# Attention steps reordered, sample scores in every step, the last head from wide to narrow, output weights split earlier, projection tiles prepared two ahead

## The chip, the cores and the metric

The kernel runs on one core of one Trainium2 chip. The metric is the device time of one execution in microseconds (us). A step below is one of the 32 rounds of the attention loop; a tile is 128 rows of tokens. The engines are TensorE (PE, its weight loads PEld), VectorE (DVE), ScalarE (ACT), GpSimd (POOL), and SyncE (SP), which here only issues DMAs.

## What is computed

One layer on a prompt of 1024 tokens and on a sample group of 8 sequences with 8 new tokens each, all in float32. The model width is 1024.

```python
z = rmsnorm(x) @ w_in                       # q, k, v for 4 heads (2 x 64 wide), u and v_a of the gate
s1, s2 = q1 @ k1.T / 8 + rel, q2 @ k2.T / 8 + rel
o_b = (softmax(s1) - lam * softmax(s2)) @ v     # causal for the prompt; 8 cached pages of 128 keys per sample
o_b = rmsnorm(o_b) * (1 - lambda_init)          # per head
o_a = u * (tril(w_s) @ layernorm(v_a) + b)      # inside chunks of 128
x = x + rmsnorm(concat(o_b, o_a) @ w_out)
h = rmsnorm(x) @ w_up; c = causal conv of width 3 over h; x = x + rmsnorm((silu(g) * u) @ w_down)
```

The outputs are the new x, the keys, values and gate rows of the new tokens, and the last two rows of h.

## The kernel before

Every large product is made from three passes of a split: a number is `hi` (rounded to the matmul's fp32r) plus a remainder `lo`, and hi*hi + hi*lo + lo*hi is accumulated. So each operand is prepared by a cast on ACT (`hi`) and a subtraction on DVE (`lo`).

The program has five stages in a row: input projection (to 290 us), attention (290 to 507), output projection with `w_out` (507 to 640), the convolution FFN (640 to about 1460) and the final norm. The order of all instructions is written out by hand, engine by engine; engines are held together by counting semaphores (`wait_ge`), and each engine works off its own list in order.

**Attention.** Step i = 8h + b works on head h and query block b. Its width is the number of 128-key blocks that it attends to, b + 1 before: 1 to 8 in every head. A step is spread over three rounds of the loop: `scores(i)` on PE (L1724, the bias on top L1732), for each of the two softmax maps a row maximum on DVE (`row_max`, L1313) and an exponential on ACT (`exponent`, L868), then `mix(i)` on DVE (L1326); one round later `turn(i)` transposes the mixed matrix on PE (L1747) and ACT copies it to SBUF (`take_turned`, L878); two rounds later `weigh(i)` multiplies with v (L1757), and `out_square` (ACT, L884), three small POOL instructions and `out_norm` (DVE, L1333) make the normalized output. `scores(i+1)` waits for both exponentials of step i, and `weigh(i)` waits for `out_norm(i-1)`, since they share a bank of PSUM.

In between stands the work on the sample group. In every step PE transposes two cached key pages (`turn_key`, L1778), one of which ACT and one DVE copies to `kt` (L858, L1342). In every second step `smp_scores` (L1798) multiplies four of them with the sample queries, 512 columns at a time. After four units `smp_softmax`, `smp_factors` and `smp_turn` (L1806) follow, and `smp_weigh` (L1821) multiplies with the value pages in two steps that follow each other: steps 10 and 11, 18 and 19, 26 and 27 before, with widths 3 and 4. Transposed keys, transposed outputs (`turn_out`, L1769, every fourth step, copied by `take_out`, L892) and turned matrices share two PSUM banks in turn (`ring`): each waits until what stood in the ring two places before it has been copied.

SP's queue holds the loads of the key pages, the value pages and `w_out` (eight blocks k of 128 rows, `wo_raw`) in the order in which they are written, and waits inside it.

**Output projection.** `out_products(t, k)` (L1878) makes six matmuls of 512 columns for tile t and block k; a tile has 48 of them. For each tile ACT copies `res` to `act_lo` as hi (`split_ahead`, L934), DVE subtracts (`split_rest`, L1424), ACT copies hi to `act_hi` (`split_place`, L939). The blocks of `w_out` are split by `split_w_out` (ACT L946, DVE L1429). After the product of a tile: square sum (ACT L1004), a root on POOL, `y_nrm`, `x_mid` (DVE), square sum (L1014), `x2_nrm`, then transposes for the FFN (`turn_x2`, PE L1870), placed behind the product of two tiles later, and their split. After tile 0 the rest of the sample attention is made, with `norm_rows` on DVE (L1406 to L1412).

The attention loop of PE in short:

```python
for i in range(NSTEP + 2):
    scores(i); turn_key(2 * i); turn_key(2 * i + 1)
    # smp_turn, smp_weigh, turn_out in some steps
    if i % 2 == 0 and i >= 2: smp_scores(i // 2 - 1)
    turn(i - 1); weigh(i - 2)
```

## Time and profile before

| | |
|---|---|
| median of 3 runs | 1487.48 us (1487.22 to 1487.87) |
| the profiled execution | 1489.29 us, span 1487.6 us |
| PE busy | 1402.0 us, 94% of the span, 8706 instructions |
| weight loads (PEld) | 1260.7 us, 85% |
| DVE, ACT, POOL busy | 718.7 (48%), 460.7 (31%), 176.5 us (12%) |
| chain that ended last | PE 88%, DVE 4%, ACT 2%, POOL 2%, issue 2%, DMA 1% |
| mean DMA rate | 78 GB/s |

The span is what the profiler sees between the first and the last instruction; 1.7 us of the profiled execution lie around it. A matmul's end is modelled, so a busy PE is not a PE at its peak: starts of instructions are the safer marks. "Granted clock" is the share of TensorE's full clock (2.4 GHz) in a stretch, 1.00 or, where part of it was at 1.2 GHz, less.

### The profile page before, as it was taken

How to read it: one execution, taken by the hardware profiler on the slowest of the kernel's cores; microseconds unless marked ns; L12 is line 12 of the kernel's file. 1: busy time of each engine (PE TensorE's matmuls, PEld its weight loads, DVE VectorE, ACT ScalarE, POOL GpSimd, SP SyncE). 2: the span in 40 equal slices, each digit the busy share in tenths (PEclk: the TensorE clock that was granted, in tenths of full speed). 3: DMA queues.
4: the chain of work that ended last, by engine and by line, in shares of the span. 5: the costliest groups of instructions: out<-in, count | busy, mean ns of one | idle time of the engine just before them, and what ended most of it. 6: DMA issues, size and time to landing. Idle time of an engine off the chain costs nothing.

```text
span 1487.6 us, 22289 instructions
## 1 busy us (share of the span) xinstructions
PE 1402.0 (94%) x8706; PEld 1260.7 (85%) x8706; DVE 718.7 (48%) x1065; ACT 460.7 (31%) x763; POOL 176.5 (12%) x320
## 2 busy tenths in 40 slices
PE   6999999989889789999999999999999999999983
PEld 5999999857666667789898989898989898989872
DVE  5333321365655644445545454536363635454547
ACT  4421021054555524334232323232323232313131
POOL 2253000111111111020000000000000000000017
PEclk9999999999999999999999999999999999999996
DMA  7202031264565423121111111010101010101006
GB/s 236 69 29 61 29 107 56 95 195 133 165 185 187 140 84 114 53 89 56 59 35 50 50 35 56 28 56 28 56 28 56 28 56 28 56 28 57 0 29 222
DMA packets 94152, 116.31 MB, mean 78 GB/s; under 512 B 6524, under 2 KB 65317, under 8 KB 94085
## 3 DMA queue, kind: packets, MB, share of 16 engines
q1 hardware_dynamic: 92277, 112.25, 23.8%
q10 hardware_dynamic: 1760, 3.01, 0.6%
q8 instruction: 44, 0.72, 0.2%
q14 instruction: 23, 0.19, 0.0%
q0 software_dynamic: 48, 0.13, 0.0%
HBM read 100.69 MB, written 14.69 MB: 78 GB/s over the span
## 4 chain that ended last, share of the span: by engine, by line
PE 88%; DVE 4%; ACT 2%; POOL 2%; issue 2%; DMA 1%; SPq 0%; DVEq 0%; ACTq 0%; POOLq 0%
PE PS L1921 36%; PE PS L1959 17%; PE PS L1664 16%; PE PS L1878 6%; PE PS L1724 3%; PE PS L1757 2%; PE PS L1732 1%; PE PS L1778 1%; POOL y_acc L1183 1%; PE PS L1821 1%; DVE small L1313 1%; PE PS L1747 1%; PE PS L1798 1%; ACT junk L1004 1%; PE PS L1652 1%
## 5 line engine op out<-in xcount | busy, mean ns | idle before, releaser
L1921 PE MATMUL PS<-act_hi,wu_hi 128*128 128x364 f32 x1056 | 347.7, 329 | 3.6 <-DVE wu_lo L1477 2.6
L1921 PE MATMUL PS<-act_lo,wu_hi 128*128 128x364 f32 x1056 | 347.7, 329 | 0.0
L1921 PE MATMUL PS<-act_hi,wu_lo 128*128 128x364 f32 x1056 | 347.4, 329 | 0.0
L1530 DVE TENSOR_TENSOR y_acc<-y_acc,PS 128x512 f32<-128x512 f32 (+1 forms) x198 | 135.1, 685 | 141.3 <-PE PS L1959 137.9
L1921 PEld LDWEIGHTS PS<-act_hi,wu_hi 128*128 128x128 f32 x1056 | 199.1, 189 | 4.3 <-DVE wu_lo L1477 2.7
L1921 PEld LDWEIGHTS PS<-act_lo,wu_hi 128*128 128x128 f32 x1056 | 199.1, 189 | 0.4
L1921 PEld LDWEIGHTS PS<-act_hi,wu_lo 128*128 128x128 f32 x1056 | 199.2, 189 | 0.0
L1959 PE MATMUL PS<-wd_hi,g_hi 128*128 128x512 f32 x360 | 143.4, 398 | 0.0
L1959 PE MATMUL PS<-wd_hi,g_lo 128*128 128x512 f32 x360 | 142.8, 397 | 0.0
L1959 PE MATMUL PS<-wd_lo,g_hi 128*128 128x512 f32 x360 | 141.7, 394 | 0.0
L1058 ACT CAST g_hi<-conv 128x1088 fp32r<-128x1088 f32 x22 | 24.3, 1104 | 275.7 <-PE PS L1959 219.3
L1171 POOL COPY stT<-hsw 128x32 f32 (+1 forms) x22 | 12.6, 572 | 738.9 <-DVE conv L1564 738.9
L1553 DVE SCALAR_TENSOR_TENSOR conv<-h_gate,cwi,conv 128x1023 f32<-128x1023 f32 x22 | 28.2, 1284 | 147.7 <-ACT conv L1048 147.7
L1664 PE MATMUL PS<-act_hi,w_hi 128*128 128x364 f32 x288 | 96.0, 333 | 0.0
L1664 PE MATMUL PS<-act_lo,w_hi 128*128 128x364 f32 x288 | 94.7, 329 | 0.0
L1664 PE MATMUL PS<-act_hi,w_lo 128*128 128x364 f32 x288 | 94.6, 328 | 0.0
L1959 PEld LDWEIGHTS PS<-wd_hi,g_hi 128*128 128x128 f32 x360 | 67.5, 188 | 21.1 <-DVE y_acc L1530 6.3
L1664 PE MATMUL PS<-w_hi,act_hi 128*128 128x256 f32 x288 | 82.0, 285 | 0.4 <-DVE act_lo L1222 0.2
L1959 PEld LDWEIGHTS PS<-wd_hi,g_lo 128*128 128x128 f32 x360 | 67.6, 188 | 16.4
L1664 PE MATMUL PS<-w_hi,act_lo 128*128 128x256 f32 x288 | 81.0, 281 | 0.0
L1664 PE MATMUL PS<-w_lo,act_hi 128*128 128x256 f32 x288 | 80.5, 280 | 0.0
L1959 PEld LDWEIGHTS PS<-wd_lo,g_hi 128*128 128x128 f32 x360 | 67.6, 188 | 14.6
(236 smaller groups left out, 2360.2 us busy)
## 6 DMA issues: line engine op xcount, KB each, us to landing
wu_raw<-in_w_up_dram SPq DMA_DIRECT2D x44, 512.0 KB, 3.9
kpage<-in_cache_k_dram SPq DMA_DIRECT2D x64, 256.0 KB, 2.9
vpage<-in_cache_v_dram SPq DMA_DIRECT2D x64, 256.0 KB, 3.1
wd_raw<-in_w_down_dram SPq DMA_DIRECT2D x22, 512.0 KB, 5.2
w_raw<-in_w_in_dram SPq DMA_DIRECT2D x20, 512.0 KB, 4.6
x_in<-in_x_prompt_dram SPq DMA_DIRECT2D x8, 512.0 KB, 6.0
wo_raw<-in_w_out_dram SPq DMA_DIRECT2D x8, 512.0 KB, 5.6
x_res<-in_x_prompt_dram SPq DMA_DIRECT2D x8, 512.0 KB, 4.1
```

The source lines that it names most:

```text
L1004: nc.scalar.activation(junk2[0:r, :], PS[0:r, j:j + 2, :].rearrange("p a b -> p (a b)"), ACT.Square, accum_out=ssq2[0:r, t:t + 1]).then_in ...
L1058: nc.scalar.copy(g_hi[:, e, :], conv[:, 1, :]).then_inc(g_hi_ready, 1)
L1183: nc.gpsimd.tensor_tensor(y_acc[0:r, t, :], y_acc[0:r, t, :], x_back[0:r, t % 3, :], ALU.add).then_inc(fout_ready, 1)
L1313: nc.vector.tensor_reduce(nmax[:, i % 4, m:m + 1], score_cols(i, m), AX.X, ALU.max, negate=True).then_inc(nmax_ready, 1)
L1530: nc.vector.tensor_tensor(dst, dst, PS[0:r, bank, :], ALU.add).then_inc(ybank_free, 1)
L1553: nc.vector.scalar_tensor_tensor(conv[:, half, NS + 1:], h[:, NS:NTOK - 1], w1, conv[:, half, NS + 1:], ALU.mult, ALU.add).then_inc(tap1_r ...
L1664: mm = nc.tensor.matmul(out, lhs, rhs, start=(i == 0), stop=(i == len(pairs) - 1))
L1724: nc.tensor.matmul(score_cols(i, m)[:, c:e], qT[d, h, qs], kT[d, h, NS + c:NS + e], start=True, stop=biased >= e)
L1757: mm = nc.tensor.matmul(PS[:, out_bank(i), 0:DV], at_sb[:, i % 2, P * k:P * k + P], v_all[:, k, DV * h:DV * h + DV], start=(k == 0), stop= ...
L1878: mm = nc.tensor.matmul(PS[:, Y_BANK[t % 2] + half, :], a[:, k, wide(t)], w[:, 512 * half:512 * half + 512], start=(k == 0 and j == 0), st ...
L1921: mm = nc.tensor.matmul(PS[:, 3 * half + c, 0:CW], a[:, half, k, :], b[:, k, CHUNKS[c]], start=(j == 0), stop=(j == len(parts) - 1))
L1959: mm = nc.tensor.matmul(PS[:, 6 + half, :], g[:, e, wide(t)], w[:, e, 512 * half:512 * half + 512], start=(j == 0), stop=(j == len(parts) ...
```

## The change

The same products are made; only their order, their grouping and one place in SBUF change.

- **Widths.** `width(i)` is still 1 to 8 in heads 0 to 2, and 8 to 1 in head 3 (steps 24 to 31).
- **Keys.** `keys_of(i)`: step 0 transposes four pages, steps 1 to 30 two each, one step earlier than before, step 31 none. ACT now copies the first (even) page of a step and DVE the second (odd) one.
- **Ring.** In every fourth step the transposed outputs come before the keys, on PE and on ACT (`take_out` before `take_keys` and the exponentials).
- **Sample scores.** `smp_scores` runs in every step on two pages, 256 columns, in place of four pages in every second one. `smp_turn` and the first `smp_weigh` stand in steps 9, 17 and 28, the second in 10, 18 and 29; the sample softmax stands in steps with i % 4 = 3.
- **Output weights.** Blocks 3, 2 and 5 of `w_out` are split at the end of steps 29, 30 and 31, block 4 in round 32, the others behind. The first tile is split in two halves of k. Tile order is 7, 6, ..., 0, 8, and the first tile takes its blocks in the order 5, 4, 3, 2, 1, 6, 7, 0.
- **Two ahead.** `split_ahead(2)` stands before the tile loop, and in the loop ACT places tile t + 2 before it waits for the product of tile t, where it placed tile t + 1 behind that product's square sum.
- **SP.** All value pages but the last two sets are loaded first; then, behind the scores of step 23, blocks 0 to 2, keys, blocks 3 to 5, keys, and the last two sets of value pages.

```diff
+    def width(i):
+        return i % QB + 1 if i // QB < H - 1 else QB - i % QB
...
+    SMP_STEP = [9, 17, 28]
+    ZERO_STEP = [8, 16, 28, 32]
+    def keys_of(i):
+        return range(4) if i == 0 else range(2 * i + 2, min(2 * i + 4, 4 * 2 * NB))
     ring, ring_taken = [], []
     for i in range(NSTEP + 1):
-        if i < NSTEP:
-            for n in (2 * i, 2 * i + 1):
-                ring.append(("key", n))
-                ring_taken.append((kt_ready[n % 2], n // 2 + 1))
-        if i % OB == 3 and i >= 7:
+        if i < NSTEP and i % OB == 3 and i >= 7:
             ring.append(("out", (i - 7) // OB))
             ring_taken.append((ot_taken, (i - 7) // OB + 1))
+        for n in keys_of(i):
+            ring.append(("key", n))
+            ring_taken.append((kt_ready[n % 2], n // 2 + 1))
         if i >= 1:
             for t in range(turns_before(i - 1), turns_before(i)):
...
+    TILES = [7, 6, 5, 4, 3, 2, 1, 0, 8]
+    WO_SPLIT = [3, 2, 5, 4, 1, 6, 7, 0]
+    FIRST_K = [5, 4, 3, 2, 1, 6, 7, 0]
...
-        for pr in range(NB // 2):
+        for pr in range(NB // 2 - 1):
             load_keys(4 * pr + 2)
             load_keys(4 * pr + 3)
-            if pr == NB // 2 - 1:
-                sp.wait_ge(score_ready, 2 * QB * (H - 1))
-                load_w_out(range(3))
             load_values(2 * pr)
-            if pr < NB // 2 - 1:
-                load_keys(4 * pr + 4)
-            else:
-                load_w_out(range(3, 6))
+            load_keys(4 * pr + 4)
             load_values(2 * pr + 1)
-            if pr < NB // 2 - 1:
-                load_keys(4 * pr + 5)
+            load_keys(4 * pr + 5)
+        sp.wait_ge(score_ready, 2 * QB * (H - 1))
+        load_w_out(range(3))
+        load_keys(2 * NB - 2)
+        load_w_out(range(3, 6))
+        load_keys(2 * NB - 1)
+        load_values(NB - 2)
+        load_values(NB - 1)
...
         def split_w_out(k):
             act.wait_ge(wo_loaded[k // 6], 16 * (6 if k < 6 else 2))
-            if k == 0:
-                act.wait_ge(rows_stored, 16 * STEPS)
-                act.wait_ge(o_ready, NSTEP)
+            if k < 4:
+                act.wait_ge(o_ready, NSTEP - 2 * k)
...
                 exponent(i, 1)
             if i == 2:
                 own_exponent()
-            if i < NSTEP and i % OB == 3 and i >= 7:
-                take_out((i - 7) // OB)
-            if i < NSTEP and at == 6 and pr >= 0:
-                smp_take(pr)
+            if i in SMP_STEP:
+                smp_take(SMP_STEP.index(i))
             if 1 <= i <= NSTEP:
                 take_turned(i - 1)
-            if i >= 4 and at in (0, 4):
-                smp_exponent(pr, at // 4)
-                if at == 4:
-                    part_exponent(pr)
-        split_ahead(0)
+            if i < NSTEP and i % 4 == 3:
+                smp_exponent(i // 8, i // 4 % 2)
+                if i % 8 == 7:
+                    part_exponent(i // 8)
+            if i == 29:
+                split_w_out(3)
+            if i == 30:
+                split_w_out(2)
+            if i == 31:
+                split_w_out(5)
+            if i == NSTEP:
+                split_ahead(0, slice(4, KD))
+                split_w_out(4)
+                split_ahead(0, slice(0, 4))
+                split_place(0, slice(4, KD))
+        split_w_out(1)
+        split_place(0, slice(0, 4))
+        split_w_out(6)
+        split_w_out(7)
         split_w_out(0)
-        split_place(0)
-        split_w_out(1)
-        split_w_out(2)
         out_square(NSTEP - 1)
-        for k in range(3, KD):
-            split_w_out(k)
         smp_take(NB // 2 - 1)
         split_ahead(1)
         take_out(NSTEP // OB - 1)
         split_place(1)
+        split_ahead(2)
         def x2_hi(t):
             for h in range(2):
                 act.wait_ge(xt_ready, 2 * STEPS + 2 * t + h + 1)
                 src = PS[:, TURN_BANK[(2 * t + h) % 4], :].rearrange("p (k t) -> p k t", k=4)[:, :, 0:rows(t)]
-                nc.scalar.copy(act_hi[:, 4 * h:4 * h + 4, cols(t)], src).then_inc(xt_hi_ready, 1)
+                nc.scalar.copy(act_hi[:, 4 * h:4 * h + 4, cols(TILES[t])], src).then_inc(xt_hi_ready, 1)
         def wu_hi_first(half):
...
             r, j = rows(t), Y_BANK[t % 2]
-            if 1 <= t < STEPS - 1:
-                split_ahead(t + 1)
+            if t + 2 < STEPS:
+                split_place(t + 2)
+            if t + 3 < STEPS:
+                split_ahead(t + 3)
...
-            if 1 <= t < STEPS - 1:
-                split_place(t + 1)
             if t == STEPS - 1:
...
         def split_w_out(k):
-            dve.wait_ge(wo_hi_ready, k + 1)
+            dve.wait_ge(wo_hi_ready, WO_SPLIT.index(k) + 1)
             nc.vector.tensor_tensor(wo_lo[k][:], wo_raw[k][:], wo_hi[:, k, :].bitcast(F32), ALU.subtract).then_inc(wo_lo_ready, 1)
...
             if 1 <= i <= NSTEP:
                 mix(i - 1)
+            if i in ZERO_STEP and i >= 28:
+                zero_values()
             if i < NSTEP:
                 row_max(i, 0)
-                take_keys(2 * i)
+            odd_keys = [n for n in keys_of(i) if n % 2 == 1]
+            for n in odd_keys[:1]:
+                take_keys(n)
+            if i < NSTEP:
                 row_max(i, 1)
+            for n in odd_keys[1:]:
...
-        split_rest(0)
-        for k in range(KD):
+            if i - 1 in SMP_STEP:
+                take_rows(SMP_STEP.index(i - 1))
+            if i == 29:
+                split_w_out(3)
+            if i == 30:
+                split_w_out(2)
+            if i == 31:
+                split_w_out(5)
+            if i == NSTEP:
+                split_rest(0, slice(4, KD))
+                split_w_out(4)
+                split_rest(0, slice(0, 4))
+                smp_factors(NB // 2 - 1)
+        for k in (1, 6, 7, 0):
             split_w_out(k)
-            if k == 3:
-                out_norm(NSTEP - 1)
+        out_norm(NSTEP - 1)
         split_rest(1)
+        split_rest(2)
...
-        def smp_scores(u):
+        def smp_scores(j):
+            u = j // 2
             pr, c, b2 = unit(u)
+            ks = slice(2 * P * (j % 2), 2 * P * (j % 2) + 2 * P)
             for i in range(2):
-                pe.wait_ge(kt_ready[i], 2 * u + 2)
+                pe.wait_ge(kt_ready[i], j + 1)
             if b2 == 0 and u >= 2:
                 pe.wait_ge(sprob_ready, u // 2)
             for h in range(H):
-                mm = nc.tensor.matmul(PS[32 * h:32 * h + 32, SMP_BANK, :], qp[:, 2 * pr + b2, h, :], kt[:, u % 2, h, :],
-                                      start=(b2 == 0), stop=(b2 == 1))
+                mm = nc.tensor.matmul(PS[32 * h:32 * h + 32, SMP_BANK, ks], qp[:, 2 * pr + b2, h, :], kt[:, u % 2, h, ks],
+                                      start=(j % 4 == 0), stop=(j % 4 == 3))
...
@@ -1827,28 +1884,28 @@
             mm.then_inc(pv_ready, 1)
         for i in range(NSTEP + 2):
-            pr, at = (i - 4) // 8, (i - 4) % 8
             if i < NSTEP:
                 scores(i)
-                turn_key(2 * i)
-                turn_key(2 * i + 1)
-            if i < NSTEP and at == 6 and pr >= 0:
-                smp_turn(pr)
-            if i < NSTEP and at == 7 and pr >= 0:
-                smp_weigh(2 * pr + 1)
             if i < NSTEP and i % OB == 3 and i >= 7:
                 turn_out((i - 7) // OB)
+            for n in keys_of(i):
+                turn_key(n)
+            if i in SMP_STEP:
+                smp_turn(SMP_STEP.index(i))
+            if i - 1 in SMP_STEP:
+                smp_weigh(2 * SMP_STEP.index(i - 1) + 1)
             if i == 1:
                 pe.wait_ge(v_kept, 2)
                 own_scores()
-            if i % 2 == 0 and i >= 2 and i <= NSTEP:
-                smp_scores(i // 2 - 1)
+                smp_scores(0)
+            if 1 <= i < NSTEP:
+                smp_scores(i)
             if 1 <= i <= NSTEP:
                 turn(i - 1)
             if i >= 2:
                 weigh(i - 2)
-            if i < NSTEP and at == 6 and pr >= 0:
...
-                    mm = nc.tensor.matmul(PS[:, Y_BANK[t % 2] + half, :], a[:, k, wide(t)], w[:, 512 * half:512 * half + 512],
-                                          start=(k == 0 and j == 0), stop=(k == KD - 1 and j == 2))
+                    mm = nc.tensor.matmul(PS[:, Y_BANK[t % 2] + half, :], a[:, k, wide(TILES[t])], w[:, 512 * half:512 * half + 512],
+                                          start=(first and j == 0), stop=(last and j == 2))
             return mm
         for t in range(STEPS):
-            pe.wait_ge(act_ready, t + 1)
+            if t >= 1:
+                pe.wait_ge(act_ready, t + 2)
             if t >= 2:
                 pe.wait_ge(ynrm_ready, t - 1)
-            if t == STEPS - 1:
-                pe.wait_ge(xt_lo_ready, 2 * STEPS + 2)
-            for k in range(KD):
+            for j, k in enumerate(FIRST_K if t == 0 else range(KD)):
                 if t == 0:
-                    pe.wait_ge(wo_lo_ready, k + 1)
-                if t == 0 and k == 6:
+                    pe.wait_ge(wo_lo_ready, WO_SPLIT.index(k) + 1)
+                    pe.wait_ge(act_ready, 1 if j < 2 else 2)
+                if t == 0 and j == KD - 1:
                     smp_turn(NB // 2 - 1)
-                mm = out_products(t, k)
```

The order of the instructions as the two programs are built, at three places (line numbers and buffer numbers are each kernel's own). First ACT, the end of the attention loop of the kernel before: `at_sb` is the copy of a turned matrix, `s_prob` the sample exponential, `L884` the square sum of an output, `wo_raw_112` to `wo_raw_119` the blocks 0 to 7 of `w_out`.

```order
L878 COPY at_sb<-PS 128x512 x2
L904 ACTIVATE s_prob_110,stat<-PS,stat 128x512
L910 ACTIVATE stat<-stat 128x3
L884 ACTIVATE PS,small<-PS,small 128x128
L934 CAST act_lo<-res 128x8x128
L946 CAST wo_hi<-wo_raw_112 128x1024
L939 CAST act_hi<-res 128x8x128
L946 CAST wo_hi<-wo_raw_113 128x1024
L946 CAST wo_hi<-wo_raw_114 128x1024
L884 ACTIVATE PS,small<-PS,small 128x128
L946 CAST wo_hi<-wo_raw_115 128x1024
L946 CAST wo_hi<-wo_raw_116 128x1024
```

The same place in the changed kernel (`wo_raw_113` to `wo_raw_120` are blocks 0 to 7 here, and the first tile comes as `128x4x128`, half of its k):

```order
L923 ACTIVATE s_prob_111,stat<-PS,stat 128x512
L929 ACTIVATE stat<-stat 128x3
L970 CAST wo_hi<-wo_raw_118 128x1024
L903 ACTIVATE PS,small<-PS,small 128x128
L897 COPY at_sb<-PS 128x128
L953 CAST act_lo<-res 128x4x128
L970 CAST wo_hi<-wo_raw_117 128x1024
L953 CAST act_lo<-res 128x4x128
L959 CAST act_hi<-res 128x4x128
L903 ACTIVATE PS,small<-PS,small 128x128
L970 CAST wo_hi<-wo_raw_114 128x1024
L959 CAST act_hi<-res 128x4x128
```

In between, three blocks (3, 2 and 5) are already split when round 32 begins, the first in step 29.

Second ACT in the projection, tiles 0 and 1: `junk<-PS` is the square sum of a product, `junk<-x_mid` the later one, `act_lo<-res` is `split_ahead`, `act_hi<-res` is `split_place`. Before:

```order
L1004 ACTIVATE junk_136,small<-PS 128x1024
L1014 ACTIVATE junk_136,small<-x_mid 128x1024
L934 CAST act_lo<-res 128x8x128
L1004 ACTIVATE junk_136,small<-PS 128x1024
L939 CAST act_hi<-res 128x8x128
L1014 ACTIVATE junk_136,small<-x_mid 128x1024
L934 CAST act_lo<-res 128x8x128
L1004 ACTIVATE junk_136,small<-PS 128x1024
L939 CAST act_hi<-res 128x8x128
```

Changed:

```order
L953 CAST act_lo<-res 128x8x128
L959 CAST act_hi<-res 128x8x128
L953 CAST act_lo<-res 128x8x128
L1041 ACTIVATE junk_137,small<-PS 128x1024
L1049 ACTIVATE junk_137,small<-x_mid 128x1024
L959 CAST act_hi<-res 128x8x128
L953 CAST act_lo<-res 128x8x128
L1041 ACTIVATE junk_137,small<-PS 128x1024
L1049 ACTIVATE junk_137,small<-x_mid 128x1024
L959 CAST act_hi<-res 128x8x128
L953 CAST act_lo<-res 128x8x128
```

Every `act_hi<-res` now stands in front of a square sum of a product and belongs to the tile after the next; tile 2 is copied ahead before the first square sum.

Third PE in step 15 (width 8), from its last biases to `weigh(13)`: `kpage` are the keys, `o_nrm` the transposed outputs, `kt,qp` the sample scores, `prob` the matrix turned. Before:

```order
L1732 MATMUL PS<-bias_hi,identr 128x256
L1732 MATMUL PS<-bias_lo,identr 128x256
L1778 MATMUL PS<-ident,kpage_91 128x128 x8
L1769 MATMUL PS<-ident,o_nrm 128x128 x4
L1747 MATMUL PS<-ident,prob_92 128x128 x7
L1757 MATMUL PS<-v_all,at_sb 128x128 x6
```

Changed:

```order
L1784 MATMUL PS<-bias_lo,identr 128x256
L1784 MATMUL PS<-bias_hi,identr 128x256
L1784 MATMUL PS<-bias_lo,identr 128x256
L1823 MATMUL PS<-ident,o_nrm 128x128 x4
L1832 MATMUL PS<-ident,kpage_101 128x128 x8
L1855 MATMUL PS<-kt,qp 32x256 x4
L1799 MATMUL PS<-ident,prob_92 128x128 x7
L1809 MATMUL PS<-v_all,at_sb 128x128 x6
L1776 MATMUL PS<-kT,qT 128x128 x2
```

The outputs have moved ahead of the keys, and four sample score matmuls of 256 columns stand in a step that had none.

## Rows read from the trace of the kernel before

**Rows 1.** Windows: us, busy us of each engine (instructions), granted clock, DMA share, GB/s

```profile
289.80:338.40 48.60, 40.84 (x310) 28.85 (x310) 31.76 (x66) 26.06 (x72) 9.24 (x19) 0.89 0.65 195
338.40:390.60 52.20, 47.66 (x461) 34.73 (x460) 31.86 (x70) 27.86 (x77) 8.04 (x24) 1.00 0.53 159
390.60:444.20 53.60, 49.06 (x459) 36.16 (x458) 31.86 (x70) 27.86 (x77) 8.04 (x24) 0.97 0.56 165
444.20:487.40 43.20, 41.23 (x418) 30.10 (x417) 25.93 (x63) 22.97 (x67) 6.81 (x21) 1.00 0.58 196
487.40:496.40 9.00, 6.42 (x48) 4.62 (x48) 5.95 (x8) 4.88 (x11) 1.22 (x3) 1.00 0.89 299
496.40:506.80 10.40, 5.69 (x48) 4.48 (x47) 5.63 (x16) 6.21 (x13) 1.87 (x6) 0.94 0.26 96
506.80:527.80 21.00, 21.00 (x215) 16.98 (x216) 9.61 (x9) 9.92 (x14) 2.71 (x4) 0.87 0.09 27
544.90:558.50 13.60, 13.56 (x49) 10.79 (x50) 4.29 (x4) 2.08 (x3) 0.75 (x2) 0.81 0.23 77
```

**Rows 2.** Waits of PE, 290 to 502 us: us in total, times, longest

```profile
PE PS L1747 <- ACT res L892: 6.8, 4, 1.7
PE PS L1747 <- DVE kt L1342: 4.3, 8, 0.6
PE PS L1757 <- DVE o_nrm L1333: 3.6, 12, 0.4
```

**Rows 3.** Waits of PE, 502 to 645 us

```profile
PE PS L1878 <- ACT act_hi L939: 12.1, 7, 5.8
PE PS L1878 <- DVE wo_lo L1429: 4.5, 1, 4.5
```

**Rows 4.** Timeline between two tiles: start, us, engine, line

```profile
572.05 1.04 PE L1870 MATMUL PS<-ident,x_nrm 128*128 128x128 f32 x8
```

**Rows 5.** Chain that ended last, from one tile to the next: start, us

```profile
573.36 0.94 ACT act_hi L939
574.35 11.42 PE PS L1878 x48
```

**Rows 6.** Timeline of step 15, width 8

```profile
381.59 1.99 PE L1724 MATMUL PS<-kT,qT 64*128 64x512 f32 x8
...
388.77 0.55 PE L1747 MATMUL PS<-ident,prob 128*128 128x128 f32 x3 [1.69 <-ACT res L892]
...
390.59 0.49 PE L1724 MATMUL PS<-kT,qT 64*128 64x128 f32 x4
```

**Rows 7.** Timeline of step 12, width 5

```profile
363.50 1.35 PE L1724 MATMUL PS<-kT,qT 64*128 64x512 f32 x8
...
366.72 1.06 PE L1798 MATMUL PS<-kt,qp 128*32 128x512 f32 x8
366.83 0.59 ACT L858 COPY kt<-PS 128x512 f32<-128x512 f32 x1 [2.66 <-PE PS L1778]
367.00 0.81 DVE L1313 TENSOR_REDUCE small<-PS 128x1 f32<-128x640 f32 x1
...
368.09 0.80 ACT L868 ACTIVATE prob<-PS,small 128x640 f32<-128x640 f32 x1
```

**Rows 8.** Timeline of step 26, the sample weights on PE

```profile
457.26 1.90 PE L1806 MATMUL PS<-c_mat,s_prob 128*128 128x64 f32 x16
...
460.93 1.93 PE L1821 MATMUL PS<-vpage,s_at 128*8 128x128 f32 x64
```

**Rows 9.** Timeline of the first two steps, DMA issues and PE

```profile
290.92 9.18 SPq L672 DMA_DIRECT2D kpage<-in_cache_k_dram  x8
...
294.67 1.23 PE L1724 MATMUL PS<-kT,qT 64*128 64x256 f32 x4 [2.87 <-ACT prob L868]
```

**Rows 10.** Split of one block of w_out on ACT and DVE: ns least/median/most

```profile
L946 ACT CAST wo_hi<-wo_raw x8: 1032/1042/1052, 502.4 to 512.5; 128x1024 fp32r<-128x1024 f32 x8
L1429 DVE TENSOR_TENSOR wo_lo<-wo_raw,wo_hi x8: 1211/1218/1226, 505.4 to 515.4; 128x1024 fp32r<-128x1024 f32 x8
```

More of the change, by code:

```diff
@@ L951, in _ @@
         for i in range(NSTEP + 2):
-            pr, at = (i - 4) // 8, (i - 4) % 8
             if i >= 3:
                 out_square(i - 3)
+            if i < NSTEP and i % OB == 3 and i >= 7:
+                take_out((i - 7) // OB)
+            for n in keys_of(i):
+                if n % 2 == 0:
+                    take_keys(n)
             if i < NSTEP:
-                take_keys(2 * i + 1)
                 exponent(i, 0)
@@ L1315, in mix @@
         def mix(i):
-            w = P * (i % QB + 1)
+            w = P * width(i)
             dve.wait_ge(prob_ready, 2 * i + 2)
@@ L1704, in scores @@
         def scores(i):
-            h, n = i // QB, i % QB + 1
+            h, n = i // QB, width(i)
             w = P * n
@@ L1740, in turn @@
         def turn(i):
-            n = i % QB + 1
+            n = width(i)
             pe.wait_ge(mix_ready, i + 1)
@@ L1767, in turn_out @@
                 bank = 0
-            for j in range(OB):
-                mm = nc.tensor.transpose(PS[:, bank, P * j:P * j + P], o_nrm[:, (OB * g + j) % QB, :], ident[:])
+            first = min(width(OB * g), width(OB * g + OB - 1))
+            for i in range(OB * g, OB * g + OB):
+                c0 = P * (width(i) - first)
+                mm = nc.tensor.transpose(PS[:, bank, c0:c0 + P], o_nrm[:, i % QB, :], ident[:])
             mm.then_inc(ot_ready, 1)
```

102 lines of the change are left out of this document (57 added, 45 removed).

## The prediction

> **What bounds the kernel now.** I read four views. The page says that PE is busy for 94% of the span and carries 88% of the chain, so only what shortens PE's path counts. The windows then split that path at the places that the change touches [rows 1]: the four heads of attention take 48.6, 52.2, 53.6 and (43.2 + 9.0) us, then 10.4 us pass until the first matmul of the projection, in which PE works for 5.7. The reader should see two kinds of stretch: heads in which PE is busy for nine tenths, and gaps. The waits of PE name the gaps. In the projection they are 12.1 us in 7 waits for `act_hi`, the longest 5.8, and 4.5 us for the first `wo_lo` [rows 3]. In attention they are small and many: 6.8 us for `take_out`'s copy, 4.3 for a key copy, 3.6 for `o_nrm` [rows 2]. The granted clock adds a third cost: it is 1.00 in the second head, but 0.97 in the third, 0.81 for the tile behind the 5.8 us gap, and 0.87 for the first tile [rows 1]. Everything behind 640 us is untouched.
>
> **The projection, two tiles ahead.** The next tile starts 1.36 us later than PE could: `turn_x2` starts at 572.05, its 8 transposes take eight issue intervals of 0.117 (1.04 less the end of the last one, 0.94), so to 572.99, but the tile starts at 574.35, behind the `act_hi` of 573.36 [rows 4, 5]. ACT makes that copy only after the square sum of the product that has just ended. After the change the copy belongs to the tile after the next and stands before that square sum, so the wait goes; `turn_x2` stays and is now what lies between two tiles. Tiles 4 to 7 give 4 x 1.36 = 5.4. Tile 3 and tile 8 have the same wait, of which I read about 0.5 and 0.8 (the 12.1 of [rows 3] less 5.8 and less the 4.2 of four waits leaves 2.1 for both with their modelled ends; I take 1.25). Tile 2 waits for 5.8 because its subtraction stands on DVE behind `norm_rows`; it now stands before the tile loop, and 5.9 go. The tile behind that gap took 13.6 at clock 0.81 [rows 1] where the others take 11.3 from 560.8 to 572.05: 2.3 more. Sum 14.9. What is late next: product t waits for `y_nrm` of t - 2, ready 4 us behind a product of 11.3; DVE needs about 6.2 us a tile and ACT 6. That is cover enough, and behind tile 0, where `norm_rows` holds DVE for 7 us and ACT begins 2 us later than before because it now copies tile 2 first, tile 3 still finds its bank free by my count with 5 us to spare.
>
> **The tail of attention.** Before, 9.0 + 10.4 = 19.4 us pass from the scores of step 31 to the first product [rows 1]. Now step 31 has width 1. Counted from its scores: ACT has split block 2 at 0.9 and DVE at 2.1, `mix(30)` to 3.0, two row maxima to 3.5, the exponentials to 4.3, the sample maximum and exponential to 5.9, block 5 on ACT to 7.2 and on DVE to 8.4 (1.04 and 1.22 each [rows 10]), `mix(31)`, turned and copied at 9.95, then half a tile ahead (0.6), block 4 (1.04), the other half (0.6), half a tile placed (0.6): 12.8 with the hand-overs. So 6.6 less than 19.4, and PE idles in it for about 8 us, as it idled 4.7 of 10.4 before: I expect the first tile at the same low clock as now (0.87), no gain there. The other blocks come at 1.22 each from DVE while PE needs 1.4 per block, so PE does not wait for them.
>
> **The last head, wide to narrow.** The gain of the tail is paid for in steps 24 to 30. A narrow step now follows a wide one and must turn and weigh it: with transposes at 0.117 and weighing at 0.234 per block, the two widths that used to be turned and weighed behind the loop (7 and 8, 15 x 0.351 = 5.3 us) stand inside it. Step by step, each the longer of PE's sum and of the chain scores, maximum, key copy, maximum, `o_nrm`, weigh: 7.5, 7.3, 7.1, 7.7, 9.5 (with the sample block), 6.8, 5.6 = 51.5, where the seven steps 24 to 30 took 43.2 [rows 1]. So the head with its tail goes from 62.6 to 64.3: +1.7. Both ends: if the chain is nowhere longer than PE's sum, 4 less; if each of the blocks split in steps 29 to 31 delays its successor by its full 2.26 us, 4 more. I take the step count, since it is built from the same row durations as the present steps, which it gives back to 0.1 us in steps 12 and 15.
>
> **Wide steps with outputs.** Step 15 takes 9.0 us, 381.59 to 390.59, with a wait of 1.69 for `take_out`, which stands behind both exponentials [rows 6]. With the outputs first in the ring that wait goes, but the second key waits for `take_out` instead, DVE takes it only at +4.5, the second maximum ends at +6.3, `o_nrm` follows and the weighing ends at 8.1. Worth 0.9 in steps 7, 15 and 23: -2.6. In steps 7 and 23 the clock also fell (third head 53.6 against 52.2, [rows 1]); with the gap broken in two I expect it to hold: 2 x 1.5 = -3.0.
>
> **Who takes which key.** DVE used to copy the first key between its two maxima; now it copies the second, which PE finishes 0.5 us later. In step 12 ACT begins the second copy 3.33 us behind the scores' start and DVE's second maximum begins at 3.50 [rows 7]. Now the DVE copy begins at 3.33, the maximum at 3.94, the exponential (0.8 and 0.2 to read the sum) ends at 5.8 against 5.5. That is +0.3 for widths 5 and 0.2 for 6 in three heads, +0.5 in steps 2 and 3: +2.1. From width 7 on the first maximum covers it. The wait of 4.3 in [rows 2] goes, but that of `o_nrm` grows in its place.
>
> **Sample scores by halves.** Eight matmul passes of 512 columns take 1.0 us of issue [rows 7]; the sixteen halves take 0.5 per step if the price goes by columns. Bounds: 0.5 and 1.0. The nearest rows are the 64 passes of 128 columns in 1.93 us, 0.03 each [rows 8], a quarter of 0.125: by columns. So PE's sum is the same, better spread.
>
> **The sample block** moves from widths 3 and 4 to widths 2 and 3. Turning (1.9 + 0.3) and weighing (2 x 2.2 with the own keys, [rows 8]) are pure PE work. Step 11 had hidden its chain under it: it took 6.2 and would now take 5.9 without it, so 2.2 moved away give 0.3. The three steps 9 to 11 go from 19.5 to 20.6: +1.1, in two heads +2.2.
>
> **The start.** Step 0 turns four pages, and the third waits for the first copy: ACT comes to the exponential 0.7 later, beneath a PE wait of 2.87 that is already there [rows 9]. Step 1 needs the second unit of pages, issued from 290.92 at 1.15 us each [rows 9]: about 298.3 with landing, 0.8 behind need. With two sample scores at the low clock: +2.5, bounds 0.7 and 4.
>
> **Sum.** -14.9 (projection) + 1.7 (last head and tail) - 5.6 (wide steps) + 2.1 (keys) + 2.2 (sample block) + 2.5 (start) = -12.0. The profiled execution took 1489.3, its span 1487.6; it would take 1477.3, and as it lies 1.8 above the median, I forecast a median of 1475.5.
>
> **A rule weighed.** The fourth head runs at granted clock 1.00 although its steps hold transposes for a third of PE's time [rows 1]. The Trainium skill, "TensorE: Matmul & The Clock Gate", section "Part 4: PE-mode transpose", says that transposes don't count as PE-busy in the way that matmuls do, and that the full clock does not engage for them. By that rule the narrow last steps, transposes and gaps, would run at 1.2 GHz. The trace bears it out only behind gaps. It is a rival below.
>
> **Rivals.**
> 1. The clock falls in the last head from step 29 on, since PE there waits for splits on ACT and DVE. For: 0.94 and 0.87 around today's gap. Against: 1.00 while PE waits 0.4 to 0.6 at a time. PE's 14 us of work in steps 29 to 31 would take up to twice that, of which I count 9 as exposed: 1484.
> 2. The small waits of [rows 2], 14.7 in all, vanish and nothing takes their place; then keys and wide steps give 9 more: 1466. Against: `o_nrm` hangs on the second maximum, and that on the second key.
> 3. The tile loop is not two ahead in effect: ACT, late by two copies behind tile 0, stays late and one wait of about 1 us per tile remains: 14.9 shrinks to 8: 1482.
> 4. Slower: the low clock takes the whole last head. Place: steps 24 to 31. It decides where the granted clock of that head is below 0.75. PE's 41 us of work [rows 1] would grow by some 30 where nothing covers them: 1505.
> 5. The last two blocks of `w_out` come too late: they are now issued behind two sets of value pages that wait for steps 28 and 29. Against: DMAs ran at 299 GB/s in a full stretch [rows 1], and at 1.04 us per page issued they would land 4 us before need. It would cost 3: inside my range, 1478.
>
> **Chances.** My forecast (with rival 5 in its range) 0.65, its own range 1471 to 1480; rival 2 0.13; rival 1 0.10; rival 3 0.07; rival 4 0.05. The range 1467 to 1483 leaves out rival 4, half of rival 1 and of rival 2. This kernel's measurement tells 0.2%, 3 us, from no change. All but rival 4 and half of rival 1 lie below 1484.5: faster 0.90, same 0.05, slower 0.05.
>
> **What would show it.** Waits of PE for `act_hi` in the projection near zero, tile to tile 12.2 us. Step 31 to the first product about 12.8 us. Heads of about 52.9 us for the second and third, and 51.5 for steps 24 to 30. Steps 7, 15 and 23 near 8.1. If the heads are shorter than 52, I have counted the DVE chain too long; if the last head is above 56, the splits or the clock stand in the way. I am wrong in kind if the projection does not give at least 12.

## The result, and the profile after

The changed kernel takes 1474.61 us (median of 4 runs, 1474.06 to 1475.22) where the kernel before took 1487.35 (4 runs on the same chip, 1486.86 to 1487.87): ratio 0.9914, 95% interval 0.9897 to 0.9932. That is 12.7 us less; the forecast was 1475.5. Its profiled execution took 1474.49, span 1472.7.

First the windows that answer to [rows 1]: the first three heads, steps 24 to 27, step 28 in two pieces, steps 29 and 30, step 31 up to the first product, tile 0, and tile 2 with what follows it. Columns as in [rows 1].

```profile
289.70:338.70 49.00, 41.04 (x360) 28.37 (x360) 31.51 (x70) 26.93 (x73) 9.22 (x19) 0.97 0.68 208
338.70:391.50 52.80, 48.66 (x493) 35.31 (x492) 31.96 (x71) 28.24 (x78) 8.24 (x24) 1.00 0.53 161
391.50:444.20 52.70, 48.56 (x491) 35.24 (x490) 31.87 (x71) 28.14 (x78) 8.25 (x24) 1.00 0.58 181
444.20:474.00 29.80, 27.32 (x210) 19.79 (x209) 20.37 (x38) 17.21 (x41) 4.22 (x12) 1.00 0.36 125
474.00:481.00 7.00, 5.79 (x48) 4.41 (x47) 2.41 (x5) 2.23 (x8) 0.85 (x3) 1.00 0.00 0
481.00:486.90 5.90, 5.55 (x87) 4.28 (x85) 1.49 (x4) 2.38 (x9) 1.00 (x4) 0.71 0.01 3
486.90:499.20 12.30, 11.22 (x149) 8.27 (x145) 6.05 (x13) 6.26 (x16) 1.68 (x3) 1.00 0.66 199
499.20:510.80 11.60, 5.62 (x38) 3.88 (x36) 8.03 (x19) 7.70 (x22) 3.20 (x6) 0.79 0.83 265
510.80:531.60 20.80, 20.80 (x215) 16.85 (x215) 9.61 (x18) 9.49 (x16) 4.09 (x7) 0.87 0.27 92
542.80:555.80 13.00, 13.00 (x66) 10.82 (x65) 8.18 (x10) 4.91 (x7) 4.84 (x6) 1.00 0.22 78
```

The chain through the projection (start, us), which answers to [rows 5]: product and `turn_x2` (L1927) alternate and nothing stands between them.

```profile
510.77 12.40 PE PS L1935 x42
...
531.58 22.48 PE PS L1935 x96
554.06 0.87 PE PS L1913 x8
554.93 0.87 PE PS L1927 x8
555.80 11.16 PE PS L1935 x48
566.97 0.87 PE PS L1927 x8
567.84 11.13 PE PS L1935 x48
```

The waits of PE up to 502 us, then from 502 to 635, which answer to [rows 2, 3]:

```profile
PE PS L1809 <- DVE o_nrm L1368: 14.6, 21, 1.1
PE PS L1776 <- ACT prob L887: 3.1, 2, 2.4
PE PS L1832 <- ACT res L911: 1.4, 6, 0.2
PE PS L1855 <- ACT s_prob L923: 1.0, 1, 1.0
...
PE PS L1799 <- DVE prob L1361: 4.3, 2, 3.8
PE PS L1978 <- DVE wu_lo L1529: 2.6, 1, 2.6
PE PS L1935 <- ACT act_hi L959: 1.1, 1, 1.1
```

`take_out` and the key copy have nearly left the first list, and `o_nrm` stands there with 14.6 where it had 3.6. In the second list 12.1 us for `act_hi` have become 1.1, before the first product. The first matmul of the feed-forward part starts at 632.32 instead of 644.87, 12.55 sooner. The two profiled spans differ by 14.9; the other 2.3 lie at the last product of the feed-forward part. In the products ahead of it PE's starts keep their distance within 0.1 us. The last one starts at 1439.19 before and at 1426.18 now, 13.0 apart; the 5 us from there, before and changed:

```profile
1439.19:1444.19 5.00, 5.00 (x12) 3.94 (x13) 2.06 (x3) 1.15 (x2) 0.00 (x1) 0.50 0.00 0
1426.18:1431.18 5.00, 5.00 (x19) 4.08 (x20) 3.32 (x6) 1.75 (x3) 0.60 (x2) 0.87 0.01 3
```

The granted clock was 0.50 in the one and 0.87 in the other, and the two are 14.7 apart behind it. The change leaves the order of this part alone. The time behind the start of the feed-forward part was 841.0 to 844.1 us in the five profiles with the attention order of before (before, e1, e7, e8, e10) and 839.1 to 840.9 in the seven with the changed one; whether the order has a hand in this is not shown. The medians, 12.7 apart, leave little for it beside the 12.5 up to the feed-forward part. So each verdict is read from the starts of steps, too, which repeat to 0.03 us from one kernel to the next where nothing is changed, but for steps 0 and 1.

**Where the time went**, term by term (starts of the scores, of the products and of the feed-forward part in both traces):

| term | forecast | measured |
|---|---|---|
| projection, first product to feed-forward | -14.9 | 138.1 to 121.55: -16.6 |
| steps 24 to 30 | +8.3 | 43.1 to 55.0: +11.9 |
| step 31 to the first product | -6.6 | 19.4 to 11.5: -7.9 |
| steps 7, 15, 23 | -5.6 | 30.0 to 24.6: -5.4 |
| who takes which key | +2.1 | +0.8 per head, steps 2 and 3 +0.5: +2.8 |
| sample block, steps 9 to 11, 17 to 19 | +2.2 | 19.55 to 20.64, twice: +2.2 |
| start, steps 0 and 1 | +2.5 | +1.4 |
| steps 8 and 16 | none | 5.50 to 5.07: -0.9 |
| sum | -12.0 | -12.5 |

### The profile page after: what moved, and what is told of

Same layout as the page of the kernel before. It is cut to its first block, busy times and chain, and to the rows that moved or that the text cites. A ratio compares the mean times of both kernels' runs of the same rounds, so it can differ in the third digit from the quotient of the medians.

```text
span 1472.7 us, 22577 instructions
## 1 busy us (share of the span) xinstructions
PE 1399.6 (95%) x8834; PEld 1259.0 (85%) x8834; DVE 718.0 (49%) x1066; ACT 461.9 (31%) x765; POOL 179.1 (12%) x320
## 4 chain that ended last, share of the span: by engine, by line
PE 89%; DVE 4%; issue 2%; POOL 2%; ACT 1%; DMA 1%; SPq 1%; DVEq 0%; ACTq 0%; POOLq 0%
PE PS L1978 36%; PE PS L2016 17%; PE PS L1716 16%; PE PS L1935 7%; PE PS L1776 2%; PE PS L1809 2%; PE PS L1832 2%; PE PS L1784 1%; DVE small L1348 1%; PE PS L1878 1%; POOL y_acc L1218 1%; PE PS L1704 1%; PE PS L2025 1%; DMA sub_gain<-in_subln_gain_dram 0%; PE PS L1863 0%
```

## The experiments

Medians; the ratio is to the kernel before, measured on the same chip (1487.81 for e1 to e4, 1487.03 for e5 to e8, 1487.92 for e9 and e10). The last three columns are read from the traces: the time of each of the first three heads (8 steps each), the time from the start of step 24 to the first product of the projection ("to product"), and from there to the first matmul of the feed-forward part ("projection").

| run | us (lowest to highest) | ratio to before, 95% interval | heads 1, 2, 3 | to product | projection |
|---|---|---|---|---|---|
| before | 1487.35 | | 48.6, 52.1, 53.7 | 62.5 | 138.1 |
| changed | 1474.61 | 0.9914 (0.9897 to 0.9932) | 48.9, 52.8, 52.8 | 66.5 | 121.6 |
| e1 | 1472.13 (1472.07 to 1472.52) | 0.9899 (0.9882 to 0.9915) | 48.8, 52.1, 53.7 | 62.5 | 121.9 |
| e2 | 1491.39 (1489.77 to 1494.39) | 1.0029 (1.0018 to 1.0040) | 49.3, 52.8, 52.8 | 66.5 | 137.8 |
| e3 | 1473.12 (1472.92 to 1473.46) | 0.9906 (0.9890 to 0.9923) | 49.8, 52.8, 52.8 | 63.0 | 121.7 |
| e4 | 1472.76 (1470.41 to 1473.69) | 0.9898 (0.9882 to 0.9915) | 50.0, 52.8, 52.8 | 63.6 | 121.6 |
| e5 | 1470.25 (1468.81 to 1470.91) | 0.9887 (0.9871 to 0.9904) | 47.6, 51.2, 51.2 | 65.4 | 121.4 |
| e6 | 1468.62 (1467.59 to 1471.73) | 0.9882 (0.9862 to 0.9901) | 47.2, 50.5, 50.5 | 68.3 | 120.6 |
| e7 | 1463.59 (1462.79 to 1465.97) | 0.9839 (0.9823 to 0.9855) | 44.7, 50.9, 50.9 | 62.2 | 121.3 |
| e8 | 1465.63 (1460.12 to 1467.34) | 0.9858 (0.9839 to 0.9878) | 44.4, 50.6, 50.6 | 61.0 | 120.7 |
| e9 | 1462.36 (1460.74 to 1464.13) | 0.9827 (0.9809 to 0.9846) | 47.6, 51.2, 51.2 | 60.2 | 120.7 |
| e10 | 1463.24 (1463.05 to 1465.64) | 0.9837 (0.9819 to 0.9855) | 45.5, 50.9, 50.9 | 60.4 | 123.1 |

### e1 and e2: two tiles ahead alone, and undone alone

```diff
 # e1, ScalarE's tile loop of the kernel before; VectorE's split_rest likewise
-            if 1 <= t < STEPS - 1:
-                split_ahead(t + 1)
+            if t + 2 < STEPS:
+                split_place(t + 2)
+            if t + 3 < STEPS:
+                split_ahead(t + 3)
             ...square sum of y...
-            if 1 <= t < STEPS - 1:
-                split_place(t + 1)
```

> The kernel before with one part of the change: the activations' split of the projection two tiles ahead (placed and subtracted before the square sum); order of tiles, attention and output weights as before. Theory A (the gain is the projection's waits alone): 1.36 us a tile, the 5.8 us wait of tile 2 and the slow tile behind it go, 14 to 17 us less than before, 1470.5 to 1473.5; first product to feed-forward part 121 to 123 us where it is 138. Theory B (the gain of the projection needs the changed tile order or the weights split early): 8 us or less, 1479 or more.

> The changed kernel with that part undone: split one tile ahead, placed behind the square sum, all else as changed. Theory A: 14 to 17 us more than the changed kernel, so 1489 to 1492, and thus slower than the kernel before by the 2 to 4 us that its attention costs more. Theory B: 8 us more or less, 1483 at most.

e1 took 15.7 us off the kernel before, and e2 is 16.8 above the changed kernel. Theory A holds in both, and the two projections (121.9 and 137.8) are those of the changed kernel and of before to 0.3 us. Two rows of e1's chain, between two tiles, and e2's wait of PE for the same place:

```profile
562.98 0.87 PE PS L1872 x8
563.85 11.14 PE PS L1880 x48
```

```profile
PE PS L1933 <- ACT act_hi L959: 13.6, 8, 6.2
```

So this one part is worth more than the whole change: e1 is 2.5 us faster than the changed kernel, and e2 is 0.3% slower than before. The rest of the change costs 2.5 us by the medians, 3.6 by the starts of steps (342.58 against 339.02 us from step 0 to the feed-forward part).

### e3: ScalarE's wait before step 28

The sample exponential behind step 27 writes a buffer whose last reader is `smp_turn` of step 17, but waited for that of step 28.

```diff
             if pr >= 1:
-                act.wait_ge(sat_ready, 2 * pr)
+                act.wait_ge(sat_ready, 2 * pr - (2 if (pr, c) == (3, 0) else 0))
```

> The changed kernel, but the sample exponential behind step 27 waits for the sample weights' turn of two blocks ago (the last reader of its buffer) and no longer for that of step 28. Theory A (step 28 takes 12.9 us instead of the 9.5 forecast because ScalarE stands in this wait, the output normalization of step 25 hangs behind it, and TensorE's clock falls in the gap): step 28 about 9.5 us at granted clock 1.00, the time 3.2 to 4 us less, 1470.6 to 1471.4. Theory B (the length of step 28 is TensorE's own work and its clock falls for another reason): under 1 us less.

The changed kernel's step 28, in which ScalarE sits idle for 5.24 us, and behind it its square sum (L903), POOL, `o_nrm` and the weighing:

```profile
478.77 0.69 ACT L923 ACTIVATE s_prob<-PS,stat 128x512 f32<-128x512 f32 x1 [5.24 <-PE PS L1867]
479.45 0.33 ACT L903 ACTIVATE PS<-PS,small 128x128 f32<-128x128 f32 x1
479.69 0.64 PE L1855 MATMUL PS<-kt,qp 128*32 128x256 f32 x8 [1.02 <-ACT s_prob L923]
481.11 0.35 DVE L1368 SCALAR_TENSOR_TENSOR o_nrm<-PS,small,sub_gain 128x128 f32<-128x128 f32 x1 [3.10 <-POOL small L1167]
```

Step 28 of e3, as a window:

```profile
475.80:485.20 9.40, 9.40 (x133) 7.52 (x132) 3.82 (x9) 4.41 (x15) 1.85 (x6) 1.00 0.00 0
```

PE is busy for all of its 9.4 us, which took 12.9 before the edit: theory A's mechanism, and the 9.5 of the forecast was the step without this wait. The median fell by only 1.5, where A said 3.2 to 4. In e3's profile, step 0 began 0.95 us later than in the changed kernel's and step 1 took 7.1 instead of 6.2; both stand ahead of the edit. Step 1, in the changed kernel, in e3, and in e7 with the old order of the keys:

```profile
295.94:302.18 6.24, 6.13 (x97) 4.51 (x98) 3.03 (x9) 1.62 (x5) 0.00 (x0) 0.73 0.77 242
296.88:304.01 7.13, 7.13 (x97) 5.32 (x97) 3.03 (x9) 1.62 (x5) 0.00 (x0) 0.57 0.75 219
295.03:300.46 5.43, 5.12 (x81) 3.90 (x81) 2.18 (x7) 1.56 (x6) 0.00 (x0) 0.69 0.71 220
```

The same step took 6.2 to 6.6 us at granted clock 0.73 to 0.74 (changed, e2, e6) and 7.0 to 7.3 at 0.56 to 0.58 (e3, e4, e5, e9), with PE busy throughout in the longer ones. So most of what varies is the clock.

### e4: output weights split behind the last step

```diff
 # ScalarE; VectorE likewise
-            if i == 29:
+            if i == NSTEP:
                 split_w_out(3)
-            if i == 30:
                 split_w_out(2)
-            if i == 31:
                 split_w_out(5)
-            if i == NSTEP:
                 split_ahead(0, slice(4, KD))
```

> The changed kernel with the three blocks of output weights that are split in steps 29 to 31 split behind the last step instead. Theory A (each split lies on the chain of its step with its 1.04 on ScalarE and 1.1 us on VectorE, as the chain of waits shows at 493 and 499 us): steps 29 to 31 together 4 to 6 us shorter, the stretch behind them about 3 longer, net 1 to 3 us faster than the changed kernel. Theory B (they lie beneath the steps' other work, so that splitting early is gain): steps unchanged, and the stretch to the first product 3 us longer, net 2 to 3 us slower.

Between the two theories. Step 29 stayed at 6.85, step 30 went from 5.48 to 4.76 and the tail from 11.53 to 10.92: 1.3 us less where A said 1 to 3 and B 2 to 3 more. The direction is A's, its sizes are not: the early splits lay on the chain in step 30 only, and the tail didn't grow, since `mix(31)`, no longer behind the subtraction of block 5, was ready sooner. Splitting early is no gain.

e4 shows one thing more. Its step 28 has the same three waits of PE as the changed kernel's (1.0, 0.8 and 0.2 us), and took 11.3 us, not 12.9. First the changed kernel's window, then e4's:

```profile
474.00:486.90 12.90, 11.34 (x132) 8.69 (x131) 3.90 (x9) 4.60 (x15) 1.86 (x6) 0.87 0.00 1
```

```profile
476.20:487.50 11.30, 9.74 (x134) 7.58 (x133) 3.89 (x9) 4.61 (x15) 1.86 (x6) 1.00 0.01 1
```

The granted clock fell to 0.87 in the one and stayed at 1.00 in the other. So the 3.5 us that the changed kernel's step 28 takes above e3's are 1.9 of waiting and 1.6 of a clock at 1.2 GHz for part of the step.

### e5 and e6: VectorE's key, and its order

```diff
 # e5: VectorE takes the even page, ScalarE the odd one
-            odd_keys = [n for n in keys_of(i) if n % 2 == 1]
+            odd_keys = [n for n in keys_of(i) if n % 2 == 0]
     (ScalarE's take_keys and the two semaphores accordingly)
 # e6: maximum, o_nrm, maximum, key
-            for n in odd_keys[:1]:
-                take_keys(n)
+            if i >= 3:
+                out_norm(i - 3)
             if i < NSTEP:
                 row_max(i, 1)
-            for n in odd_keys[1:]:
-                take_keys(n)
-            if i >= 3:
-                out_norm(i - 3)
+            for n in keys_of(i):
+                if n % 2 == 1:
+                    take_keys(n)
```

> The changed kernel with the engines' keys as before: VectorE copies the first page of a step, between its two maxima, ScalarE the second. Theory A (the second key between the maxima is what makes steps of width 5 and 6 longer): their 5.99 and 6.16 us go back to about 5.55 and 5.92, width 7 to 6.6, and 2 to 3.5 us fall off in all: 1471.1 to 1472.6. Theory B (the sample scores in every step do it, not the key): steps as in the changed kernel, no difference over 0.5 us.

> The changed kernel with VectorE's order in a step changed from maximum, key copy, maximum, output normalization to maximum, output normalization, maximum, key copy. Theory A (TensorE's 15 us of waits for the output normalization are bound by its place on VectorE): these waits fall below 4 us, steps of width 5 and 6 take 5.5 to 5.7 and 5.9 to 6.0, in all 3 to 8 us less, 1466.6 to 1471.6. Theory B (what bounds a step is the second exponential, which must be done before the next scores may overwrite its bank; the wait for the normalization only stands in for it): the waits turn into waits for the exponential or for the key copy, now late, and the time changes by less than 1.5 us.

e5: widths 5, 6 and 7 went to 5.55, 5.91 and 6.62, the steps of before to 0.02 us: theory A. It also took 0.87 off each of steps 7, 15 and 23 (8.2 to 7.3), which nobody had expected there. So the median fell by 4.4, more than A said, and the start of the feed-forward part came 5.8 sooner, counted from step 0. In step 15 of the changed kernel the second key is turned behind `take_out`, and VectorE, which has finished its maximum, idles for 0.78 before it can copy that key and come to its second maximum:

```profile
387.04 0.65 PE L1832 MATMUL PS<-ident,kpage 128*128 128x128 f32 x4 [0.24 <-ACT res L911]
387.73 0.69 DVE L1377 COPY kt<-PS 128x512 f32<-128x512 f32 x1 [0.78 <-PE PS L1832]
388.34 1.21 DVE L1348 TENSOR_REDUCE small<-PS 128x1 f32<-128x1024 f32 x1
389.96 1.58 PE L1809 MATMUL PS<-v_all,at_sb 128*128 128x128 f32 x12 [0.78 <-DVE o_nrm L1368]
```

e6: the wait for `o_nrm` nearly vanished (0.6 us in 2), width 5 fell to 5.08, below what either theory said, and the median by 6.0. Theory A, but in the narrow steps and in step 28 the late key becomes the wait, as B feared:

```profile
PE PS L1797 <- DVE kt L1377: 8.3, 13, 1.6
PE PS L1797 <- DVE prob L1361: 5.1, 2, 4.0
...
PE PS L1807 <- DVE o_nrm L1368: 0.6, 2, 0.3
```

Its step 28 took 15.2 us at granted clock 0.78, 2.3 more than in the changed kernel: a wait of 1.6 for the late key, and more of the step at the low clock.

### e7 and e8: before, with two parts of the change

```diff
 # e7, on top of e1: order of the two banks; PE and ACT accordingly
         if i < NSTEP:
+            if i % OB == 3 and i >= 7:
+                ring.append(("out", (i - 7) // OB))
+                ...
             for n in (2 * i, 2 * i + 1):
                 ring.append(("key", n))
                 ...
-        if i % OB == 3 and i >= 7:
-            ring.append(("out", (i - 7) // OB))
-            ...
```

> The kernel before with two parts of the change: tiles two ahead as in the first run, and in the steps that turn outputs (7, 15, 23, 31) the outputs first in the banks' order, in TensorE's and in ScalarE's; keys, sample scores and last head as before. Theory A (the wait for ScalarE's copy of the outputs is what makes these steps long, and it has no other side): step 15 from 9.0 to 8.2, steps 7 and 23 from 10.5 to 8.2, step 31 by 0.8: 5.5 to 6.5 us less than the first run, 1465.5 to 1467. Theory B (it needs the keys one step ahead or the split sample scores): steps 7, 15 and 23 above 8.9, under 3 us less.

> The run before this one, with VectorE's order in a step maximum, output normalization, maximum, key copy, and VectorE taking the second page, ScalarE the first. Theory A (as in the same edit of the changed kernel): steps of width 5 and 6 at or below their 5.55 and 5.92, in all 2 to 6 us less than the run before this one. Theory B: no difference over 1 us, or longer, as the ring of two banks waits for a key copied later.

e7 took 8.5 us off e1, more than A said: with the keys taken as before, steps 7, 15 and 23 take 7.3 each where I expected 8.2 (they took 10.6, 9.0 and 10.6), and only steps 11, 19 and 27 grew (6.16 to 6.62). It is 11 us faster than the changed kernel. e8 stays open. Its steps are 2.7 us shorter than e7's up to the feed-forward part, but its median is 2.0 longer, its four runs spread from 1460.1 to 1467.3, and the shortest is the profiled one. The spread goes with the mean granted clock of the runs: 0.989, 0.985, 0.983 and 0.983 for 1460.1, 1463.9, 1467.3 and 1467.3 us. Where the longer runs lost it no trace shows.

### e9 and e10: the two ways to end attention

e9 is e3, e4 and e5 together. e10 is e7 with the following:

```diff
         split_rest(0)
         for k in range(KD):
             split_w_out(k)
+            if k == 0:
+                smp_factors(NB // 2 - 1)   # stood ahead of split_rest(0)
+                zero_values()
```

> The changed kernel with three edits of the runs before together: the sample exponential behind step 27 freed, the keys copied by the engines as before, output weights split behind the last step. Theory A (the three prices are separate terms of one sum): step 28 about 9.4 us, widths 5 and 6 at 5.55 and 5.91, steps 24 to the first product 65.4 - 3.5 - 1.3 = 60.6 us, and the whole 7.5 to 9.5 us less than the changed kernel: 1465 to 1467. Theory B (removing one uncovers another, such as the splits becoming the longest wait): 6 us less or fewer.

> The kernel of run e7 (before, with tiles two ahead and outputs first), with VectorE's six small operations and the clearing of a bank for the last sample pair moved behind the subtractions for the first tile and the first block of output weights. Theory A (TensorE's wait of 4.5 us for the first low part of the weights is VectorE's queue, in which these operations stand first): first product 1.5 to 2 us sooner, the time 1.5 to 2.5 us less than e7, 1461 to 1462. Theory B (ScalarE's copies set it): first product within 0.5 us of e7's, no difference. Beside e9 it also compares the two ways of ending attention: wide last head and no early splits here, 62.2 us from step 24 to the first product, less 1.8; narrow last there, 60.6.

e9: the terms add up (step 28 at 9.40, widths 5 and 6 at 5.55 and 5.92, 60.2 us to the product), and 1462.36 is 12.3 us below the changed kernel, nearly 3 more than the upper end of A. In the trace the feed-forward part starts 11.7 sooner, counted from step 0: 6.3 between step 24 and the product, 4.6 in the three heads, for which A's range had left 1.6 to 3.6, and 0.8 in the projection. e10: the first product came 1.8 us sooner, as A said, but the time did not move (1463.24 to e7's 1463.59). PE's wait for the first low part is down from 4.5 to 2.7 us, and 1.1 for the second is new, as its subtraction now stands behind the moved operations. Behind that second wait the products are issued every 0.43 us, the low level, where the six before it took 0.23 each: the gap was moved into the first tile, and the projection grew by 1.8.

```profile
497.92 0.48 PE L1883 MATMUL PS<-wo_hi,act_hi 128*128 128x512 f32 x1 [2.69 <-DVE wo_lo L1430]
498.23 0.40 PE L1883 MATMUL PS<-wo_lo,act_hi 128*128 128x512 f32 x1
...
499.16 0.52 PE L1883 MATMUL PS<-wo_hi,act_lo 128*128 128x512 f32 x1
500.80 0.79 PE L1883 MATMUL PS<-wo_hi,act_hi 128*128 128x512 f32 x1 [1.12 <-DVE wo_lo L1430]
501.39 0.63 PE L1883 MATMUL PS<-wo_lo,act_hi 128*128 128x512 f32 x1
501.82 0.63 PE L1883 MATMUL PS<-wo_hi,act_lo 128*128 128x512 f32 x1
```

The two ways to end attention, at their best here: 60.2 us to the product with the last head reversed, 60.4 with the widest step last. Counted on to the feed-forward part, past the gap that e10 moved, it is 180.9 (e9) against 183.5 (e10; e7 also 183.5, e8 181.7). In heads 1 to 3 it is e10 that is shorter, by 2.6. The kernels differ in more than the order of the last head (keys a step ahead, sample scores by halves, the place of the sample block, the first tile in halves), and no run reverses the head alone, so what the reversal by itself is worth isn't shown. e9 and e10 are 12.3 and 11.4 us faster than the changed kernel and 1.7 and 1.6% faster than before, and their times don't tell them apart.

## Why the prediction was right, and where it was not

**The mechanism of the gain was right, its size 1.7 too small.** Forecast 12.2 us from tile to tile, measured 12.03, against 13.56 before. Each of four tiles gave 1.53 instead of 1.36. The product is issued in the same 11.25 us in both kernels; by starts `turn_x2` takes 0.79 between two products, where I had 0.94:

```profile
566.81 1.03 PE L1927 MATMUL PS<-ident,x_nrm 128*128 128x128 f32 x8
567.60 0.48 PE L1935 MATMUL PS<-wo_hi,act_hi 128*128 128x512 f32 x1
```

From the start of tile 1 to that of tile 3, with the wait of 5.8 and the slow tile behind it, 9.1 us went (forecast 5.9, 2.3 and half a microsecond of tile 3's wait), and tile 8 gave 1.1 (forecast 0.8). One reading of mine was off without harm: the four waits of before are 1.26 each, 5.0 in all and not 4.2, which leaves 0.39 and 0.84 for tiles 3 and 8, the 1.25 that I had taken. e1 and e2 show that the part stands alone.

**The step that failed is one of the seven in the last head: "9.5 (with the sample block)".** It took 12.9, and the head 55.0 instead of 51.5. I had added up PE's work, and the chain through VectorE, but not followed ScalarE's queue in order. With the block moved from step 26 to step 28, the sample exponential that ScalarE issues at the end of step 27 stands before the `smp_turn` that it waits for, and the square sum of step 25 is queued behind it. e3 removes the wait and gets 9.4. The wait is 1.9 of the 3.4 us by which the step was missed; the rest is the low clock, which e4 did not have behind the same waits. The other six steps came out within 0.12 us (7.54, 7.41, 7.05, 7.77, 6.86, 5.48).

**The tail** was 1.3 shorter than forecast: I had the sample exponential at 5.9 us behind the scores of step 31, and it ended at 5.0 (504.20), so block 5 and `mix(31)` came sooner. That splitting blocks early serves the tail was wrong (e4).

**The wide steps** came out as forecast (8.2, forecast 8.1), and for the reason given, the second key behind `take_out`. But this was no price of moving the outputs: with the first key on VectorE they take 7.3 (e5, e7). I had priced the two edits one beside the other and missed that their product was 0.87 in each of three steps.

**The start** cost 1.4, not 2.5. Step 0 grew by 1.35, and step 1 took 6.24 as before (6.23). But before's step 1 ran at granted clock 0.51 and this one at 0.73. At nearly like clock (0.69) e7's, with the old order of the keys, took 5.43, 0.8 less, and the changed kernel's variants at 0.56 to 0.58 took 7.0 to 7.3. So a price of that size is there, and in this profile the clock hid it, which is luck. Little of it is the landing that I had put it down to: the weight load for the page waited 0.3 us for its DMA here. Step 1 now also holds two sets of sample scores, 97 matmuls where e7 has 81.

**By halves at a little over half the price**: eight passes of the sample scores are now issued in 0.57 us per step (367.62 to 368.19 in step 12), where [rows 7] had 1.0 for twice the columns. Priced nearly by columns; I had taken 0.5.

**The rivals.** Rival 1 (the clock falls from step 29 on) had its mechanism in the wrong place: steps 29 and 30 ran at 1.00, and it fell in step 28, behind PE's waits there. Rival 2 fell: the small waits turned into 14.6 us for `o_nrm`. Rival 3: no wait per tile is left. Rival 4, the low clock over the last head, didn't come; 1.00 from 444.2 to 481.0 and from 486.9 to 499.2. Rival 5: PE waited for no block of `w_out`. On the rule weighed: the narrow steps ran at full clock here, too: from 486.9 to 499.2 us 23 transposes (16 of keys, 7 of probabilities) are 3.3 of PE's 11.2 busy us, at granted clock 1.00. The longest stretch of transposes alone in this trace is 26 of them in 2.9 us (626.84 to 629.73), also at 1.00, so a longer one is not tested. As far as it goes, this trace again does not bear out the sentence of the Trainium skill, "TensorE: Matmul & The Clock Gate", "Part 4: PE-mode transpose".

That the sum came out within 0.5 us is luck: +2.3 for the last head with its tail and +0.7 for the keys stand against -1.7 for the projection, -1.1 for the start, and -0.9 in steps 8 and 16, which I had not looked at. By the terms it was right in its main part, the projection, and 3.4 us off in step 28.

## What to carry to other kernels

When a block of work is moved along a step table, write down for every engine what stands in its queue behind each wait that the move touches; a sum of work and one dependence chain don't show an in-order engine that stands still. Measure the parts of a combined change apart: here one part gives 16 us alone and a second 8.5 beside it, and the whole change gives 12.7. And two edits which touch the same chain (who copies a key, and what is turned ahead of it) are priced together.

## What the runs showed of the hardware

The granted clock did not answer alike to like gaps: two kernels with the same waits in the same step (2.0 us in all) had 0.87 and 1.00. A stretch is therefore priced with both levels, and only a window of the run itself tells which it had. Nor did it behind the gap at the end of attention: the first 5 us of products ran at 0.50 in before, the changed kernel, e1, e3 and e4, at 0.54 in e7, at 0.64 in e10, where the second wait stands in them, and at 0.67 in e8 and e9. Before, e1, e7 and e8 have the same wait of 4.5 us for `wo_lo` ahead of them. A window of e7:

```profile
499.00:504.00 5.00, 5.00 (x13) 3.96 (x14) 3.64 (x4) 5.00 (x8) 2.71 (x4) 0.55 0.00 0
```
